# Chunk signals one by one, wide narrow-sum matmuls, a split reciprocal and a reordered router stage in a two-layer hybrid decoder trunk

## The reference

```
c_act = silu(c)
for l in range(2):
    sh1, sc1, g1, sh2, sc2, g2 = split(c_act @ ada_w[l] + ada_b[l], 6)
    h = rmsnorm(x, norm_mix_w[l]) * (1 + sc1) + sh1
    proj = h @ w_in[l]          # conv branch, linear recurrence, spatial gating, three gates
    x = x + g1 * (merged(proj) @ w_o[l])
    h = rmsnorm(x, norm_ffn_w[l]) * (1 + sc2) + sh2
    if l == 0: ffn = (silu(h @ w1) * (h @ w3)) @ w2              # 1024 -> 2816 -> 1024
    else:      logits = h @ router_w + router_b                  # 8 experts
               top2 = top_k(logits, 2); gates = softmax(top2)
               ffn = sum_e gates[e] * swiglu_e(h)                # each 1024 -> 2816 -> 1024
    x = x + g2 * ffn
return rmsnorm(x, final_norm_w)
```

## Time and profile before

| what | value |
|---|---|
| timed runs, median | 1558.95 us |
| the profiled execution's own time | 1555.98 us |
| its span, first to last instruction | 1554.2 us |
| mean granted TensorE clock | 0.992 |
| PE busy | 1529.3 us (98%) |
| DVE busy | 1292.5 us (83%) |
| ACT busy | 954.9 us (61%) |
| DMA, mean | 302 GB/s |

### The profile page before, as it was taken

How to read it: one execution, slowest core, us unless ns; L and a number is a source line. 1 busy time by engine, 2 the same in 40 slices (tenths; PEclk the granted TensorE clock), 3 DMA queues, 4 the chain that set the end, 5 groups by cost and what they waited for, 6 DMA issues and landing times.

```text
span 1554.2 us, 26495 instructions
## 1 busy us (share of the span) xinstructions
PE 1529.3 (98%) x9663; PEld 1319.3 (85%) x9663; DVE 1292.5 (83%) x1507; ACT 954.9 (61%) x1103; POOL 39.5 (3%) x46
## 2 busy tenths in 40 slices
PE   8999999999999999999999999999999999999998
PEld 8999999999999998999977777777777777777775
DVE  7896878777774796878689999999888998989898
ACT  3535544444434524544478787777877778787785
POOL 0000000000000000000020000000000000000200
PEclk8999999999999999999999999999999999999999
DMA  9943879388984643989479999999999999999993
GB/s 348 311 144 122 272 272 311 109 271 285 324 304 132 204 136 109 343 282 375 140 256 385 389 382 396 388 382 380 382 364 388 367 381 383 362 384 368 392 391 159
DMA packets 260769, 469.01 MB, mean 302 GB/s; under 512 B 15748, under 2 KB 129596, under 8 KB 260692
## 3 DMA queue, kind: packets, MB, share of 16 engines
q1 hardware_dynamic: 257168, 456.75, 82.7%
q0 software_dynamic: 3248, 11.11, 2.0%
q10 hardware_dynamic: 276, 0.09, 0.0%
HBM read 453.90 MB, written 14.00 MB: 301 GB/s over the span
## 4 chain that ended last, share of the span: by engine, by line
PE 87%; DVE 7%; issue 2%; DMA 2%; ACT 1%; SPq 1%; DVEq 0%; ACTq 0%
PE psU L647 62%; PE psA L647 23%; DVE split L1408 2%; PE psA L1094 1%; DMA raw<-in_w_in_dram 1%; DVE adacc L1486 1%; DMA raw<-in_ada_w_dram 1%; DVE sc L1661 0%; DVE work L1728 0%; PE psU L1053 0%; DVE rstd L1520 0%; DVE work L1776 0%; DVE merged L1526 0%; DVE work L1645 0%; DVE work L1638 0%
## 5 line engine op out<-in xcount | busy, mean ns | idle before, releaser
L1179 ACT ACTIVATE split<-raw 128x1024 fp32r<-128x1024 f32 x750 | 784.3, 1059 | 362.5 <-PE psU L647 168.9
L1905 DVE TENSOR_TENSOR split<-raw,split 128x1024 fp32r<-128x1024 f32 x528 | 615.4, 1218 | 23.1 <-ACT split L1179 22.0
L647 PE MATMUL psU<-split,xE 128*104 128x512 f32 (+1 forms) x2304 | 497.1, 375 | 1.0 <-DVE xE L2032 1.0
L647 PE MATMUL psU<-hS,split 128*128 128x256 f32 x3840 | 471.4, 284 | 8.6 <-DVE hS L1612 4.7
L647 PEld LDWEIGHTS psU<-hS,split 128*128 128x128 f32 x3840 | 464.7, 192 | 11.7 <-issue 5.7
L647 PEld LDWEIGHTS psU<-split,xE 128*104 128x104 f32 x2304 | 366.0, 168 | 119.0 <-issue 1.4
L1408 DVE TENSOR_TENSOR split<-raw,split 128x1024 fp32r<-128x1024 f32 x222 | 264.0, 1218 | 65.3 <-ACT split L1179 64.7
L647 PE MATMUL psA<-split,hidE 128*104 128x512 f32 x1056 | 249.3, 395 | 0.0
L647 PEld LDWEIGHTS psA<-split,hidE 128*104 128x104 f32 x1056 | 175.4, 168 | 64.0
L1486 DVE SCALAR_TENSOR_TENSOR adacc<-raw,cact,adacc 128x1024 f32<-128x1024 f32 x56 | 71.8, 1281 | 3.6
L647 PE MATMUL psU<-yS,split 128*128 128x256 f32 x576 | 70.1, 283 | 0.0
(11 more groups left out here) (255 smaller groups left out, 865.6 us busy)
## 6 DMA issues: line engine op xcount, KB each, us to landing
raw<-in_moe_w_dram SPq DMA_DIRECT2D x528, 512.0 KB, 7.3
raw<-in_w_in_dram SPq DMA_DIRECT2D x116, 512.0 KB, 5.5
raw<-in_ada_w_dram SPq DMA_DIRECT2D x96, 512.0 KB, 7.2
raw<-in_ffn_w_dram SPq DMA_DIRECT2D x66, 512.0 KB, 7.1
raw<-in_w_o_dram SPq DMA_DIRECT2D x16, 512.0 KB, 8.7
token_rows<-sc SPq DMA_DIRECT2D x10, 512.0 KB, 9.3
raw<-in_w_br_a_dram SPq DMA_DIRECT2D x8, 512.0 KB, 8.5
raw<-in_w_br_c_dram SPq DMA_DIRECT2D x8, 512.0 KB, 8.7
```

The lines of the kernel that those rows point to most:

```text
L647: return pe.matmul(o, a, b, start=start, stop=stop, skip_group_check=True)
L1179: return act.activation(o, i, ACT.Copy)
L1905: TTN(split[:, slot, 1, :], raw[:, (RAW0 + n) % RAW, :], split[:, slot, 0, :].bitcast(F32), ALU.subtract).then_inc(s_lo, 1)
```

## The change

What it does, in the order of the program:

1. SP interleaves the four `whole` pieces with the second eight modulation pieces, one `whole` piece after each two, instead of all four ahead of them.
2. `direct_piece` and `half_section` use 64 equal moving columns where they had one; DVE reads every 64th column. The fill before `start_units` goes from 8 to 6 matmuls.
3. In all norms but the router's, a chunk is signalled by itself; `norm_low` makes one chunk and stands behind each chunk but the first two. PE's first unit (or first pair of the dense channel mixer) takes both output halves of a chunk k before the next k.
4. In the mixers one low part is made after `keep_scores(l, 5)`, ahead of `prepare(l, 7)`, and the reciprocal of 1024 columns becomes two of 512 with one low part between.
5. In the router stage the logits use 64 moving columns (the router's 8, eight times). The last turn of x (`xtok` 3) goes ahead of `rank`. `rank` has four matmuls for five, and the gate vector is spread by transposes. DVE picks experts before it makes any low part of the first item; the list of items is made with fewer steps. The gathered tokens are signalled and rounded in two halves. The fill of 4 before the item loop goes. ACT's two sigmoids of the gates move into the first item.

The core of the diff:

```diff
@@ sync
-                if pos == WHOLE_AT:
-                    for n in range(4):
+                if pos in WHOLE_AT:
+                    for n in WHOLE_AT[pos]:
@@ constants
-FILL_NORM, FILL_LOGITS, FILL_ITEM = 6, 2, 4
-FILL_X, FILL_SCALE, FILL_SUM, FILL_SHIFT, FILL_CHUNK = 6, 5, 4, 3, 8
+FILL_NORM, FILL_LOGITS = 6, 2
+FILL_X, FILL_SCALE, FILL_SUM, FILL_SHIFT, FILL_CHUNK = 6, 5, 4, 3, 6
-WHOLE_AT = len(START) // 2 - 1
+WHOLE_AT = {len(START) // 2 - 1 + (0, 2, 4, 6)[n]: [n] for n in range(4)}
+WIDE = 64
@@ tensor, project (the same in dense_ffn)
+                        order = [(m, kk) for m in range(2) for kk in range(4)]
+                        if chunk and j == 0:
+                            order = [(m, kk) for kk in range(4) for m in range(2)]
@@ tensor, direct_piece and half_section
-                        last = mm(bank[:, m:m + 1], raw[:, pos % RAW, (4 * kk + m) * P:(4 * kk + m + 1) * P],
-                                  cact[:, 2 * p + kk:2 * p + kk + 1], kk == 0 and m == 0, False)
+                        last = mm(bank[:, m * WIDE:(m + 1) * WIDE], raw[:, pos % RAW, (4 * kk + m) * P:(4 * kk + m + 1) * P],
+                                  cact[:, 2 * p + kk:2 * p + kk + 1].to_broadcast([P, WIDE]), kk == 0 and m == 0, False)
-                    last = mm(bank[:, m:m + 1], acc[:, (4 * h + m) * P:(4 * h + m + 1) * P], ones[:, 0:1],
+                    last = mm(bank[:, m * WIDE:(m + 1) * WIDE], acc[:, (4 * h + m) * P:(4 * h + m + 1) * P], ones[:, 0:WIDE],
@@ tensor, router stage
-                    last = mm(bank[:, tt * NE:(tt + 1) * NE], merged[:, k, tt * P:(tt + 1) * P], rtw[:, k, :],
+                    last = mm(bank[:, tt * 8 * NE:(tt + 1) * 8 * NE], merged[:, k, tt * P:(tt + 1) * P],
+                              rtw[:, k:k + 1, :].to_broadcast([P, 8, NE]), k == 0 and tt == 0, k == KD - 1)
             for j in range(4):
                 turn_rows("htok", merged, j)
+            turn_rows("xtok", xT, 3)
             bank = open_unit("rank")
-            turn_rows("xtok", xT, 3)
+                    if m % 4 == 3:
+                        last.then_inc(s_tok, 1)
             pe.wait_ge(s_uA, emptied(UNITS, len(UNITS), "A"))
-            stream(psU[3], FILL_ITEM)
             pe.wait_ge(s_items, 1)
-                        pe.wait_ge(s_xlo, i + 1)
+                        pe.wait_ge(s_xlo, i * 2 + 1)
+                            if (g, which) == (0, 0) and 2 * q == KD // per:
+                                pe.wait_ge(s_xlo, i * 2 + 2)
@@ scalar, router stage
-            for n in range(2):
-                item_high(0, n)
             for j in range(4):
                 rows_out("htok", htok, j)
+            rows_out("xtok", oacc, 3)
+            item_high(0, 0)
             for j in range(2):
                 copy(g2bc[:, j * 512:(j + 1) * 512], unit(("g2", j))[:, :]).then_inc(s_uA, 1)
-            rows_out("xtok", oacc, 3)
-            act.wait_ge(s_prob, 1)
-            act.activation(prob[:, 0:2], cur[:, 0:2], ACT.Sigmoid)
-            act.activation(prob[:, 2:4], cur[:, 0:2], ACT.Sigmoid, scale=-1.0).then_inc(s_prob, 1)
-            for n in range(2, 4):
-                item_high(0, n)
+            item_high(0, 1)
+            act.wait_ge(s_tok, 1)
+            tokens(first_rows[0], 0)
+            item_high(0, 2)
+            act.wait_ge(s_tok, 2)
+            tokens(first_rows[1], 1)
@@ vector, norm and norm_low
-                    if k in (3, 5, 7) and (l, second) != (1, 1):
-                        norm_low(l, second, k - 3)
+                    if k > 1 and (l, second) != (1, 1):
+                        norm_low(l, second, k - 2)
+            def norm_low(l, second, k):
+                dve.wait_ge(s_hh, KD * (2 * l + second) + k + 1)
+                dve.wait_ge(s_xr, KD * (2 * l + second) + k + 1)
+                sh = 24 * second + k
+                STT(hS[:, 1, k, :], merged[:, k, :], mod[:, l, sh:sh + 1], hS[:, 0, k, :].bitcast(F32),
+                    ALU.add, ALU.subtract).then_inc(s_h, 1)
@@ vector, mixer
                 keep_scores(l, 5)
+                low_parts(SIGNAL[l, "ah", 1][2] + AHEAD)
                 prepare(l, 7)
-                link(dve.reciprocal(OSD, OSD))
+                link(dve.reciprocal(half(OSD, 0), half(OSD, 0)))
+                low_parts(SIGNAL[l, "g", 0][2] + AHEAD)
+                link(dve.reciprocal(half(OSD, 1), half(OSD, 1)))
@@ vector, router stage
-            for n in range(2):
-                item_low(0, n)
+            link(dve.memset(total[:, :, :], 0.0))
...
-                link(dve.tensor_copy(ov[:, dst, 0:shift], ov[:, src, 0:shift]))
-                link(TTN(ov[:, dst, shift:NO], ov[:, src, shift:NO], ov[:, src, 0:NO - shift], ALU.add))
+                link(TTN(total[:, dst, NO:], total[:, src, NO:], total[:, src, NO - shift:2 * NO - shift], ALU.add))
...
+            item_low(0, 0)
             dve.wait_ge(s_uA, emptied(UNITS, len(UNITS), "A"))
-            dve.wait_ge(s_xhi, 1)
-            tokens_low(event("gather0"))
+            for j in range(2):
+                dve.wait_ge(s_xhi, j + 1)
+                tokens_low(psA[2 * (EVENT_AT["gather0"] % 2) + j], j)
+                if j == 0:
+                    item_low(0, 1)
```

More of the change, by code:

```diff
@@ L112, in unit_plan @@
     plan += [(("xtok", j), "A") for j in range(3)] + [("logits", "D")]
-    plan += [(("htok", j), "A") for j in range(4)] + [("rank", "D")]
-    plan += [(("g2", j), "A") for j in range(2)] + [(("xtok", 3), "A")]
+    plan += [(("htok", j), "A") for j in range(4)] + [(("xtok", 3), "A"), ("rank", "D")]
+    plan += [(("g2", j), "A") for j in range(2)]
     return plan
@@ L321, in program @@
         ov = sb("ov", [P, 8, NE * JEX])
+        total = sb("total", [P, 3, 2 * NE * JEX])
+        picked = sb("picked", [P, REX, NE * JEX])
         FB, KB, QB, GB, QT, KT, ITOK, AB, AC, AH = (work[:, j, :] for j in range(10))
@@ L670, in project @@
                         w = next_split()
-                        for m in range(2):
-                            for kk in range(4):
-                                if chunk and j == 0 and m == 0:
-                                    chunk(4 * q + kk)
-                                last = tile(bank[:, m * T:(m + 1) * T], w, 4 * q + kk, kk * 256 + m * P,
-                                            q == 0 and m == 0 and kk == 0, q == 1 and kk == 3)
+                        order = [(m, kk) for m in range(2) for kk in range(4)]
+                        if chunk and j == 0:
+                            order = [(m, kk) for kk in range(4) for m in range(2)]
+                        for m, kk in order:
+                            if chunk and j == 0 and m == 0:
+                                chunk(4 * q + kk)
+                            last = tile(bank[:, m * T:(m + 1) * T], w, 4 * q + kk, kk * 256 + m * P,
+                                        q == 0 and m == 0 and kk == 0, q == 1 and kk == 3)
                         last.then_inc(s_used, 1)
@@ L920, in dense_ffn @@
                                 stream(banks[0], FILL_NORM)
[L921 to L927 removed]
+                            order = [(m, kk) for m in range(2) for kk in range(4)]
+                            if pair == 0 and which == 0:
+                                order = [(m, kk) for kk in range(4) for m in range(2)]
+                            for m, kk in order:
+                                k = 4 * q + kk
+                                if pair == 0 and which == 0 and m == 0:
+                                    pe.wait_ge(s_h, KD + k + 1)
+                                last = tile(banks[m][:, which * T:(which + 1) * T], w, k, kk * 256 + m * P,
+                                            k == 0, k == KD - 1)
                             last.then_inc(s_used, 1)
@@ L1367, in item @@
                         item_high(i, n)
+                    if first and n == AHEAD:
+                        act.wait_ge(s_prob, 1)
+                        act.activation(prob[:, 0:2], cur[:, 0:2], ACT.Sigmoid)
+                        act.activation(prob[:, 2:4], cur[:, 0:2], ACT.Sigmoid, scale=-1.0).then_inc(s_prob, 1)
                     for g in range(len(GROUPS)):
@@ L1374, in item @@
                         act.wait_ge(s_gath, i + 1)
-                        tokens(psU[0:2])
-            item(0, 4)
+                        for j in range(2):
+                            tokens(psU[j], j)
+            item(0, 3)
+            act.wait_ge(s_items, 1)
+            n_items = act.value_load(nitem[0:1, 0:1], min_val=NE, max_val=MAXI)
             with act.Fori(1, n_items) as i:
```

116 lines of the change are left out of this document (47 added, 69 removed).

## The result

The changed kernel took 1545.81 us in the median of its four timed runs, the kernel before 1558.78 in the median of four; the ratio is 0.9916 with a 95% interval of 0.9902 to 0.9931. One of the four took 3862.4 us at a granted clock of 1.000, for a reason that nothing here shows, and it is left out of the ratio; the other three took 1543.59, 1544.82 and 1546.80 us, with a median of 1544.82. The forecast was 1546.5. The profiled execution took 1546.8 us with a span of 1544.1, against 1555.98 and 1554.2. So between the two profiles 10.1 us were won, where the sum says 12.5. I come back to why the median was met all the same.

The account below looks back on a forecast made before the run. PE, busy in nearly all of the 1554.2 us span, bounds the kernel; 2.8 + 1.0 + 0.5 + 2.2 + 0.2 + 5.8 = 12.5 us gives 1543.5, plus 2.97 from execution to median: 1546.5 us, range 1543.2 to 1551.6.

Parts of the forecast that it names:

- start: Start of the kernel: interleaved loads, full clock and single chunk signals let PE resume earlier, 2.8 us; 1.4 if clock low.
- norm 2 of layer 0: Second norm of layer 0: PE follows DVE from chunk 0 with both output halves per chunk, 1.0 us, bounds 0.8 and 1.16.
- norm 1 of layer 1: First norm of layer 1: 1.27 us of waits, about half given back, 0.5 us gained, bounds 0.3 and 1.2.
- low part ahead of prepare: Mixers, at `prepare(l, 7)`: moving one low part ahead removes PE's wait, 1.1 us in each layer, 2.2 us.
- reciprocal: Mixers: splitting it only moves the stall by two pieces; 0.2 us for both layers, bounds 0 and 2.3.
- router stage, tenth piece of the first item included: Router stage into first item: items start 7.0 us earlier, PE waits a microsecond at tenth piece; 5.8 us, bounds 4.5 and 7.0.
- the first rival: Clock falls anyway in start, router stage or both; router gain 2.7 instead of 5.8, both 1551.0 us; chance 0.22.
- if the clock changed in another place: Sign against the prediction, whole kernel: the clock changing at another place would show it wrong; no size given.
- if PE had to wait for a `whole` piece: Sign against the prediction, at the start: PE waiting for one of these pieces would show it wrong; no size given.
- the reading that this means only that records follow each other: Clock rule, argued against from the router's trace: under it the widening would bring nothing.
- with norms and reciprocals in full: Extended case of the rival that DVE is faster in item 0: 16.5 us gained, 1542.5 us; rival's chance 0.08.
- the interleaving: Rival at the start: widenings do not matter, interleaved `whole` pieces cost at most 2 us; 1551.5 us, chance 0.03.

Follow-up runs that it names:

- wide_sum: Changed kernel with 64 equal moving columns instead of one in the eleven later modulation sums too; median 1543.64 us, ratio 0.9904.
- whole_block: Changed kernel with the four `whole` pieces loaded in one block again behind the eighth modulation piece; median 1547.33 us, ratio 0.9936.
- pair_order: Changed kernel with PE's first unit in its old order, all k of output half 0 first; median 1545.33 us, ratio 0.9936.
- after_again: The changed kernel itself, unaltered, timed again in one group with `wide_early` and `best`; median 1547.75 us, ratio 0.9938.
- narrow_start: Changed kernel with one moving column instead of 64 in the start's direct pieces and half sums; median 1546.11 us, ratio 0.9916.
- narrow_logits: Changed kernel with the router's 8 columns once instead of eight times in the logits; median 1547.62 us, ratio 0.9935.
- rows_late: Changed kernel with DVE's row numbers behind the thirteenth low part of the first item instead of the ninth; median 1549.53 us, ratio 0.9932.
- no_low7: Changed kernel without the low part ahead of `prepare(l, 7)`, made behind it with three others; median 1548.77 us, ratio 0.9945.
- one_recip: Changed kernel with one reciprocal of 128x1024 instead of two halves with a low part between; median 1544.82 us, ratio 0.9929.
- wide_lows: `wide_sum` with two low parts moved earlier, one in both mixers, one behind layer 1's first norm; median 1538.62 us, ratio 0.9877.
- wide_early: `wide_sum` with low parts of the first item made in DVE's idle time and ACT's high parts earlier; median 1541.97 us, ratio 0.9897.
- best: `wide_sum` plus the moves of `wide_lows` and `wide_early` and 12 filling matmuls in PE's pause near 38.6 us; median 1534.97 us, ratio 0.9841.

## Why the prediction was right, and where not

By its own steps, profile against profile:

| step | sum | measured |
|---|---|---|
| start | 2.8 | 2.74 |
| norm 2 of layer 0 | 1.0 | 1.3 |
| norm 1 of layer 1 | 0.5 | 0.15 |
| low part ahead of prepare | 2.2 | 2.7 |
| reciprocal | 0.2 | 0.0 |
| router stage, tenth piece of the first item included | 5.8 | 3.2 |
| together | 12.5 | 10.1 |

**The step that failed** is the clock in the router stage: "at 0.115 us a record they end at 773.0", with 2.4 GHz throughout. Everything ahead of the stage came 6.9 us earlier, so the old stretch would stand at 764.5; it began at 759.2, in the second of two one-column sums that the change had left narrow and that I had not looked at, and covered the transposes and the stream ahead of the logits. Those logits ended at 769.25 and not at 766.1 (773.0 less 6.9). That is the first rival, in its router part: 2.7 instead of 5.8 for the stage, measured 3.2. Where the stretch is missing the stage gives 3.22 + 3.05 = 6.3 us against the profile before, in `wide_sum`, `whole_block` and `pair_order`; so the rest of the step, the order of DVE and the shorter list, was right within half a microsecond. The wait at the tenth piece was foreseen as "a microsecond"; it was 0.70 us and cost 0.97.

Three of the prediction's own signs came out against it. It would be wrong "if the clock changed in another place", and the clock did. The item loop was to start 12 to 13 us earlier and started 11.1 us earlier (777.28 against 788.35). It would also be wrong "if PE had to wait for a `whole` piece": PE waited 0.33 us for one at 28.83. That wait cost nothing at the end of the start, since DVE read PE's last sum at 39.36 us, where 39.35 was forecast.

**Why the median was hit.** The sum gives 1543.5 for a profiled execution, and it took 1546.8: 3.3 too low. To this I added the 2.97 us by which the median of before stood above its profile, as if that distance belonged to the kernel. It goes mostly with the granted clock of the single execution: in the last group the kernel before ran with a span of 1554.4 us at a mean granted clock of 0.994 and with 1560.3 at 0.989. The recorded median of after stood 1.0 us below its profile, and that of the other three runs 2.0. So 3.3 us too low in the sum met 4.0 (or 5.0) too high in the distance, and what was left is 0.7 (or 1.7) us. That is luck. Timed again in `after_again` the changed kernel had a median of 1547.75, 9.6 us below the kernel before in the same group; in the first timing the difference was 13.0. The median of the kernel before alone moved by 4.0 us between the groups (1556.09 to 1560.07). So the medians can't tell a gain of 12.5 us from one of 10.1; the two profiles can.

**The clock in the profiles.** Stretches at 1.2 GHz, in us, by place, without those behind 1530 us, at the very end:

| profile | 17 to 20 us | near 40 | near 291 | near 760 |
|---|---|---|---|---|
| before | 10.2 | 3.4 | - | 6.8 |
| changed, and once more | - | 3.4 | - | 6.8 |
| narrow_start | 3.4 | 6.8 | - | 3.4 |
| narrow_logits | - | 3.4 | - | 6.8 + 3.4 |
| rows_late | - | 6.8 | - | 6.8 |
| whole_block | - | 3.4 | 6.8 | - |
| pair_order | - | 6.8 | 3.4 | - |
| no_low7 | - | 6.8 | 6.8 | 6.8 |
| one_recip | - | 6.8 | - | 3.4 |
| wide_sum, wide_lows | - | 3.4 | - | - |
| wide_early | - | 6.8 | - | - |
| best | - | - | - | - |

Each of the ten profiles with one-column modulation sums has a stretch that begins near 291 or 760 us, in or right behind such sums; none of the four with 64 columns has. Sums of one column stand in other places too, near 494 us for one, where no profile has a stretch. A stretch of 6.8 us near 291 or 760 us costs 3.05 to 3.09 us, one of 3.4 us 1.4 to 1.5. This rests on profiles, ten against four, on the medians of one group, and on the mean granted clock of the timed runs: 0.996 to 0.999 in all 22 of the kernels with 64 columns, 0.992 to 0.996 in the six of `after_again`; of the runs with narrow sums, the one of 3862.4 us aside, only two reached 0.997.

PE is busy for all of the 3.50 us ahead of the fall (the row 755.70:759.20 above), as it was at the router in the kernel before. The Trainium skill, "TensorE: Matmul & The Clock Gate", Part 1, says that the clock follows how busy PE has been; the reading that this means only that records follow each other, against which the prediction argued, has this row against it too. The same part says that the same kernel meets the change at another matmul in each run. The two profiles of the changed kernel do not show that, since the clock falls at 759.2 and 759.1 us; the granted clocks of nine of its timed runs, 0.992 to 0.997, only say that not all have the same time at half clock.

**Start.** The size was right, the reason half. I held PE's sum for the end of the chain at half clock and priced the clock at 1.4 us; in `narrow_start` PE resumed on time with 3.4 us at half. What a stretch of 10.2 us would do with the new order no run shows. Shown are 1.0 us for the order of the loads; how the other 1.7 are shared among the single signals, the smaller fill and the clock no run shows. The pause near 40 us left another 1.4 us to be had, which no term of the sum looked at.

**Norms and reciprocal.** The give-back in the first norm of layer 1 was foreseen, by half, and was nearly all: 0.16 us were left, below the lower bound of 0.3. The second norm of layer 0 gave 1.28, above the upper bound of 1.16; I did not follow that, and `pair_order` leaves open what the order of the output halves is worth there. The reciprocal went as written, "the stall moves by two pieces". What I did not see is that DVE's order had room: one low part ahead of the output's products removes the stall. The prepare step was sized by the wait (1.10) and gave 1.35; I did not follow the 0.25. Among the rivals two sums are off by about 0.2 us (16.7 and not 16.5 with norms and reciprocals in full, 1551.3 and not 1551.5 for the interleaving); neither sets a bound.

## What to carry to other kernels

A stall that moves when one piece of work is split can be a stall of order: look for the instruction that the late engine needs and put it ahead of work that nobody waits for. Idle time of the splitting engine before a serial stage is the place for the next stage's first pieces. And where a kernel's time scatters, read the granted clock of several executions: one-column sums and pauses ahead of the fall were cheap to widen and to fill here, and a distance between profile and median is no constant to carry over.

## What the runs showed of the hardware that I had not expected

- A matmul with 64 equal moving columns takes nearly what one with a single column takes, at full clock: 16 records in 1.90 us against 1.84, 8 in 1.10 (row 37.52 above) against 0.95 (in `narrow_start`, at 37.66).
- The clock falls with PE busy all the time, in or behind one-column records: near 760 us in eight of the ten profiles with narrow sums, near 291 us in three of them, and in none of the four with 64 columns.
- Twelve filling matmuls in a pause of 2.56 us cost nothing, and the stretch behind the pause, which the other thirteen profiles have, was gone.
- The scatter of the times is smaller where the sums are wide: 4.2, 2.2 and 1.3 us in five or six runs each of `wide_sum`, `wide_lows` and `wide_early`, and 1.1 in `best`, against 3.6 to 7.3 in six runs each of the changed kernel, `narrow_start`, `rows_late` and `narrow_logits`.
